# Where the mLSTM's inverse roots are taken, and which rows begin the output projection

## What is computed

```python
ht = mlstm_chunkwise(mq_h, mk_h, mv_h, log_i, log_f)
ht = ht * lax.rsqrt(jnp.mean(ht * ht, axis=-1, keepdims=True) + EPS)
m_out = ht.reshape(B, S, MLSTM_W) * mh_norm_g * jax.nn.sigmoid(mo)
...
a_out = sliding_window_attention(q, k, v, attn_sinks)
y = jnp.concatenate([m_out, a_out], axis=-1)
return y @ w_out
```

## Time and profile before

| | us |
|---|---|
| median of 3 runs | 3037.35 (3036.88 to 3037.41) |
| the profiled execution | 3027.4 |
| its span, first to last instruction | 3025.7 |
| TensorE busy | 2869.6 |
| VectorE busy | 1771.5 |
| ScalarE busy | 1181.9 |
| GpSimd busy | 202.1 |

### The profile page before, as it was taken

How to read it: one execution, slowest core, us unless ns; L and a number is a source line. 1 busy time by engine, 2 the same in 40 slices (tenths; PEclk the granted TensorE clock), 3 DMA queues, 4 the chain that set the end, 5 groups by cost and what they waited for, 6 DMA issues and landing times. The chain is left out here.

```text
span 3025.7 us, 35464 instructions
## 1 busy us (share of the span) xinstructions
PE 2869.6 (95%) x14392; PEld 2397.6 (79%) x14392; DVE 1771.5 (59%) x2588; ACT 1181.9 (39%) x1737; POOL 202.1 (7%) x206
## 2 busy tenths in 40 slices
PE   8979999999988999989969999999999988899999
PEld 6637888878456888879945899999999965688887
DVE  6666766677557767657567565425534127565463
ACT  5254524434444424342245443213323235453342
POOL 1112000020112000000021100000000002100001
PEclk9989999999989999999989999999999999999999
DMA  5302333333112243325630112121121221222322
GB/s 198 104 2 90 111 118 114 95 115 123 49 36 84 94 140 95 118 68 187 234 96 26 66 56 64 53 74 63 61 58 63 63 84 43 94 88 86 110 88 80
DMA packets 84178, 271.47 MB, mean 90 GB/s; under 512 B 9264, under 2 KB 12208, under 8 KB 83632
## 3 DMA queue, kind: packets, MB, share of 16 engines
q1 hardware_dynamic: 84016, 269.21, 27.6%
HBM read 267.08 MB, written 2.10 MB: 89 GB/s over the span
## 5 line engine op out<-in xcount | busy, mean ns | idle before, releaser
L921 PE MATMUL PS<-HH,WH 128*128 128x512 f32 (+1 forms) x3032 | 1004.2, 368 | 56.0 <-DVE HL L566 20.9
L921 PE MATMUL PS<-HL,WH 128*128 128x512 f32 (+1 forms) x3032 | 997.4, 366 | 0.0
L921 PE MATMUL PS<-HH,WL 128*128 128x512 f32 (+1 forms) x3032 | 997.1, 366 | 0.0
L777 DVE TENSOR_TENSOR WL<-STAGE,WH 128x1024 fp32r<-128x1024 f32 (+2 forms) x420 | 482.6, 1150 | 518.5 <-ACT WH L771 518.0
L921 PEld LDWEIGHTS PS<-HH,WH 128*128 128x128 f32 x3032 | 562.5, 189 | 138.8 <-DVE HL L566 28.9
L771 ACT ACTIVATE WH<-STAGE 128x1024 fp32r<-128x1024 f32 (+2 forms) x420 | 407.9, 973 | 658.7 <-DMA STAGE<-in_w_down 275.4
L921 PEld LDWEIGHTS PS<-HH,WL 128*128 128x128 f32 x3032 | 562.8, 189 | 65.7
L921 PEld LDWEIGHTS PS<-HL,WH 128*128 128x128 f32 x3032 | 563.2, 189 | 65.0 <-issue 1.4
L921 PE MATMUL PS<-GH,WH 128*128 128x512 f32 (+1 forms) x880 | 294.7, 367 | 0.0
L921 PE MATMUL PS<-GL,WH 128*128 128x512 f32 (+1 forms) x880 | 294.7, 367 | 0.0
L921 PE MATMUL PS<-GH,WL 128*128 128x512 f32 (+1 forms) x880 | 294.6, 367 | 0.0
(11 more groups left out here) (236 smaller groups left out, 2564.6 us busy)
## 6 DMA issues: line engine op xcount, KB each, us to landing
STAGE<-in_w_up SPq DMA_DIRECT2D x176, 512.0 KB, 3.5
MODBUF<-in_w_mod SPq DMA_DIRECT2D x96, 512.0 KB, 4.2
STAGE<-in_w_in SPq DMA_DIRECT2D x84, 512.0 KB, 3.6
STAGE<-in_w_down SPq DMA_DIRECT2D x64, 384.0 KB, 3.1
STAGE<-in_w_down SPq DMA_DIRECT2D x64, 320.0 KB, 2.9
STAGE<-in_w_out SPq DMA_DIRECT2D x32, 512.0 KB, 4.5
BM<-in_na_bias SPq DMA_DIRECT2D x24, 256.0 KB, 3.1
CR<-in_const_ret SPq DMA_DIRECT2D x2, 1664.0 KB, 8.8
```

Source lines behind the costliest of these rows:

```text
L777: dve.tensor_tensor(WL[unit.slot][:, 0:size], STAGE[unit.slot][:, 0:size], WH[unit.slot][:, 0:size].bitcast(F32), ALU.subtract).then_inc(w ...
L921: ins = pe.matmul(self.acc(tile, col, tn), w[:, c:c + P], r[:, k, t0:t0 + tn], start=(k == 0 and m == 0), stop=(k == seg.kc - 1 and m == 2))
```

## The change

`CopyHead` gives way to `MixHead`. Inside `mix1` the steps that took the roots, spread them, multiplied by gain and gate (DVE) and by the numerator (POOL) are gone, the mixer has 20 steps instead of 22, and ACT's queue ends with a load of the table set of the logarithm. In the output projection's head, ACT takes Ln and Exp once over all 128 partitions; TensorE spreads four rows after chunk 2 of the first three tiles; DVE does the gain and also the product with the numerator, head by head. The eight chunks begin with attention's four rows, of which three are made in the mixer and the fourth in the head; the weight rows are reordered on the host to match. `NUM` moves to the rows of `Z1` that held the queries and keys before their convolution. In step 3 DVE does `weigh` ahead of `normed(0)`.

```diff
@@ -353,7 +353,7 @@
         class Head:
-            begins = False
+            begins = ready = False
             def __init__(self, hi, lo, tokens):
@@ -384,34 +384,74 @@
             def pool(self, pool):
                 pass
-        class CopyHead(Head):
-            def __init__(self, src, chunks, hi, lo, tokens):
-                super().__init__(hi, lo, tokens)
-                self.src, self.chunks = src, chunks
+        class MixHead(Head):
+            begins = ready = True
+            def __init__(self, vec, hi, lo):
+                super().__init__(hi, lo, SEQ)
+                self.vec = vec
             def copied(self, act, c):
-                n = self.tokens
-                act.activation(self.hi[:, c, 0:n], self.src[:, self.chunks[c], 0:n], ACT.Copy).then_inc(h_hi.sem, 1)
+                act.activation(self.hi[:, c, :], Z1[:, ROWS1[c], :], ACT.Copy).then_inc(h_hi.sem, 1)
             def low(self, dve, c):
-                n = self.tokens
                 self.wait_hi(dve, c)
-                dve.tensor_tensor(self.lo[:, c, 0:n], self.src[:, self.chunks[c], 0:n],
-                                  self.hi[:, c, 0:n].bitcast(F32), ALU.subtract).then_inc(h_lo.sem, 1)
+                dve.tensor_tensor(self.lo[:, c, :], Z1[:, ROWS1[c], :], self.hi[:, c, :].bitcast(F32),
+                                  ALU.subtract).then_inc(h_lo.sem, 1)
             def act(self, act):
-                for c in range(4, DC):
-                    self.copied(act, c)
+                act.activation(MEAN2, MEAN2, ACT.Ln, scale=float(D // P)).then_inc(head_ln.sem, 1)
+                self.copied(act, 3)
+                act.wait_ge(head_ln.sem, head_ln.at(1))
+                act.activation(MEAN2, MEAN2, ACT.Exp, scale=-0.5).then_inc(head_rstd.sem, 1)
+                for h in range(4):
+                    act.wait_ge(head_out.sem, head_out.at(h + 1))
+                    self.copied(act, 4 + h)
                 for u in range(3, self.run.ring):
                     self.run.split_high(act, u)
             def dve(self, dve):
-                for c in range(4, DC):
-                    self.low(dve, c)
+                def gain(h):
+                    dve.wait_ge(head_ps.sem, head_ps.at(h + 1))
+                    if later(h - 1):
+                        dve.wait_ge(head_out.sem, head_out.at(h - 1))
+                    dve.scalar_tensor_tensor(out=HG[h % 2], in0=PS[2 + h // 2][:, h % 2 * SEQ:h % 2 * SEQ + SEQ],
+                                             scalar=self.vec[:, V1_MH + h:V1_MH + h + 1], in1=Z1[:, O1 + h, :],
+                                             op0=ALU.mult, op1=ALU.mult).then_inc(hg_done.sem, 1)
+                def out(h):
+                    dve.wait_ge(hg_done.sem, hg_done.at(h + 1))
+                    dve.tensor_tensor(Z1[:, V1 + h, :], NUM[:, h, :], HG[h % 2], ALU.mult).then_inc(head_out.sem, 1)
+                self.low(dve, 3)
+                gain(0)
+                out(0)
+                for h in range(1, 4):
+                    gain(h)
+                    self.low(dve, 3 + h)
+                    out(h)
+                self.low(dve, 7)
                 for u in range(3, self.run.ring):
                     self.run.split_low(dve, u)
+            def begin(self, pe, seg):
+                first = seg.tiles[0:3]
+                for k in range(DC):
+                    if k == 3:
+                        pe.wait_ge(head_rstd.sem, head_rstd.at(1))
+                        for h in range(4):
+                            pe.matmul(PS[2 + h // 2][:, h % 2 * SEQ:h % 2 * SEQ + SEQ],
+                                      CST1[:, C1_SELB + h * P:C1_SELB + h * P + P], MEAN2,
+                                      start=True, stop=True).then_inc(head_ps.sem, 1)
+                    self.wait_lo(pe, k)
+                    for tile in first:
+                        self.run.pe_chunk(pe, tile, k)
         class RetentionHead(Head):
             begins = True
@@ -1039,7 +1079,9 @@
             if any(seg.prep for _, segments in parts for seg in segments):
                 done(qk_own=4, conv_done=12, qk_done=4, gate_ps=2, gate_in=2, abs_done=1, exp1_done=1, ln_done=1, cum_done=2, g_done=1,
                      m_done=1)
-            if parts[0][0].begins:
+            if parts[0][0].ready:
+                done(head_ln=1, head_rstd=1, head_ps=4, hg_done=4, head_out=4)
+            elif parts[0][0].begins:
                 done(mean_ps=3, centred=3, group_sq=3, var_ps=3, group_ln=3, group_rstd=3, group_out=6, gate_done=1)
...
         h1 = region(o_h, 2 * DC * TOK * 4)
         h1("ROWS_LO", [P, 4, SEQ])
         MXB = h1("MXB", [P, 4, SEQ])
-        h1("ROWS_HI", [P, 4, SEQ])
-        NUM = h1("NUM", [P, 4, SEQ])
+        h1("ROWS_HI", [P, 8, SEQ])
+        NUM = Z1[:, Q1:Q1 + 4, :]
         VT = h1("VT", [P, 4, SEQ])
         WT = [h1(f"WT{i}", [P, SEQ]) for i in range(2)]
         PT = [h1(f"PT{i}", [P, SEQ]) for i in range(2)]
...
+        head_ln, head_rstd, head_ps, hg_done, head_out = (
+            S(n) for n in ("head_ln", "head_rstd", "head_ps", "hg_done", "head_out"))
+        ROWS1 = [AQ1, AQ1 + 1, AQ1 + 2, AQ1 + 3, V1, V1 + 1, V1 + 2, V1 + 3]
...
             U = 4 * NB
             LAG = 3
-            steps = range(U + 6)
-            spread = {11: 0, 12: 1, U + 3: 2, U + 4: 3}
+            steps = range(U + LAG + 1)
...
             rotated_at = {-1: (0, 1), 0: (2, 3), 1: (4,)}
-            order = [("scores", 0)]
-            for s in steps:
-                order += [("scores", s + 1)] if s + 1 < U else []
-                order += [("spread", spread[s])] if s in spread else []
-            turn_of = {job: i for i, job in enumerate(order)}
...
-                    def wait_c(job):
-                        if later(turn_of[job] - 1):
-                            kind, x = order[turn_of[job] - 2]
-                            if kind == "scores":
-                                pe.wait_ge(p_done.sem, p_done.at(x + 1))
-                            else:
-                                pe.wait_ge(hg_done.sem, hg_done.at(x + 1))
                     def key_scores(m):
                         h, i = divmod(m, NB)
                         r = half(h % 2)
-                        wait_c(("scores", m))
-                        pe.matmul(c_bank(("scores", m))[:, 0:SEQ - i * P], QK[r, 2 + h // 2, i * P:i * P + P],
+                        if later(m - 1):
+                            pe.wait_ge(p_done.sem, p_done.at(m - 1))
+                        pe.matmul(C_PS[m % 2][:, 0:SEQ - i * P], QK[r, 2 + h // 2, i * P:i * P + P],
                                   QK[r, h // 2, i * P:SEQ], start=True, stop=True).then_inc(c_ps.sem, 1)
...
-                    def spread_rows(h):
-                        pair = half(h // 2)
-                        pe.wait_ge(hrstd.sem, hrstd.at(h // 2 + 1))
-                        wait_c(("spread", h))
-                        pe.matmul(c_bank(("spread", h)), CST1[pair, C1_SELB + h * P:C1_SELB + h * P + P], MEAN2[pair, :],
-                                  start=True, stop=True).then_inc(c_ps.sem, 1)
...
                             mean_square(s // NB - 1)
-                        if s in spread:
-                            spread_rows(spread[s])
...
-                    def rstd(p):
-                        rows = MEAN2[half(p), :]
-                        act.wait_ge(v_done.sem, v_done.at(p + 1))
-                        act.activation(rows, rows, ACT.Ln, scale=float(D // P)).then_inc(hln_done.sem, 1)
-                        act.wait_ge(hln_done.sem, hln_done.at(p + 1))
-                        act.activation(rows, rows, ACT.Exp, scale=-0.5).then_inc(hrstd.sem, 1)
...
                             squares(s // NB - 1)
-                        if s in (10, U + 2):
-                            rstd(s // (U + 2))
                         if U - 4 <= s < U - 4 + READY:
                             ahead.split_high(act, s - U + 4)
-                        if U - 3 <= s <= U:
-                            if s < U - 1:
-                                act.wait_ge(head_out.sem, head_out.at(s - U + 4))
-                            else:
-                                act.wait_ge(o_done.sem, o_done.at(NB * (s - U + 2)))
-                            ahead.first_head.copied(act, s - U + 3)
+                        if U - 3 <= s < U:
+                            c = s - U + 3
+                            act.wait_ge(o_done.sem, o_done.at(NB * (c + 1)))
+                            ahead.first_head.copied(act, c)
+                    act.preload_act_table_set("natural_log")
...
-                    def head(h):
-                        pool.wait_ge(hg_done.sem, hg_done.at(h + 1))
-                        pool.tensor_tensor(Z1[:, V1 + h, :], NUM[:, h, :], HG[h % 2], ALU.mult).then_inc(head_out.sem, 1)
...
                             sinks(a)
-                        if s in (13, 14, U + 4, U + 5):
```

(43 more changed lines are left out.)

## The result

**3005.93 us** median (3004.39 to 3006.99, 4 runs) against 3037.11 for the kernel before (3036.18 to 3037.41, 4 runs) in the same comparison: ratio 0.9896, 95% interval 0.988 to 0.9911. That is 31.2 us less; forecast were 22.8, with 3008 as the low end of the range. The direction held, the size was 8.4 us short.

What follows compares the result with a forecast made beforehand. In the mixer a ring of DVE, ACT and TensorE was taken as the bound, behind the first group TensorE; 6.7 + 6.2 + 4.2 + 5.3 + 0.4 = 22.8 us gave 3004.6 profiled, 3014.5 median, range 3008 to 3024.

Steps and rivals of the forecast that it cites:

- weigh 11 to 15: Mixer steps between those DVE weigh starts: 25.32 us in layer 0 and 24.77 in layer 1 would become 18.6.
- weigh 15 to first copy-out: Mixer's tail plus output projection's first tiles: 4.2 us gained in layer 0, 5.3 in layer 1, to 36.9 us.
- order swap: Mixer step 3, weigh ahead of normed(0): DVE's weigh no longer delays the next mask, 0.2 us a layer.
- The middle: Mid-mixer steps without the root, gain rows and POOL products fall to quiet pace: 6.7 us in layer 0, 6.2 in layer 1.
- Rival (c): Mid-mixer gives back less, step 12 to 13 staying near 7.5 us: 3019, or 3023 with head stalls; chance 0.25.
- The tail: Mixer's end: everything between attention's last store and POOL's last product goes; projection starts 0.75 us after block end, at 217.9.
- drain: Table load at block's end: skill's extra 1.38 us was not charged, only 1.28; with it, 20.0 instead of 22.8 us.
- The spreads' price: Projection's head, before chunk 3: four fp32 spreading matmuls on TensorE cost 3.6 us, not hidden.
- (d): Gain is eaten: mixer's ring takes no room back, head stalls cost 2.5 us a layer: 3033; chance 0.04.
- (e): Slower: head starves TensorE, which stays at 1.2 GHz for the whole group: 3046; chance 0.03.
- The head: Output projection's first three tiles: kept at 17.7 us, first 5.0 at 1.2 GHz, plus 3.6 for spreads.
- Rival (b): TensorE doesn't fall to 1.2 GHz between mixer and projection: 2.4 us more a layer, 3010; chance 0.18.

Runs made afterwards that it cites:

- experiment 5: Changed kernel with ACT's Ln and Exp and their two table loads back in step 10, result unused: 3015.51 us.
- experiment 6: Changed kernel with two useless POOL products a layer back in steps 13 and 14: 3009.24 us.
- experiment 7: Changed kernel with each of the head's four spreading matmuls issued twice: 3015.64 us.
- experiment 8: Changed kernel with the head's four products on POOL instead of VectorE: 3006.84 us.
- experiments 2 and 4: 2: kernel before with six useless fp32 matmuls a layer in the tail, 3029.3 us; 4: changed kernel with two more table loads ending ACT's block, 3014.75 us.
- experiment 9: Changed kernel with useless fp32 matmuls in TensorE's remaining holes in the mixer: 3002.85 us, repeated 3004.61 us.

## Why the prediction was right or wrong

The terms against the two profiles of before and the three of after (first matmul, stores and copies as in the timelines):

| | forecast | measured |
|---|---|---|
| weigh 11 to 15, layer 0 | 6.7 | 6.7, 7.3 (25.32, 25.93 to 18.65) |
| the same, layer 1 | 6.2 | 6.1, 6.7 (24.77, 25.34 to 18.65) |
| weigh 15 to first copy-out, layer 0 | 4.2 | 4.6 (mean of 41.1, 41.3 less mean of 35.3, 37.2, 37.1) |
| first to third copy-out, layer 0 | not priced | 1.1 (9.79, 9.74 to 8.75, 8.69, 8.65) |
| weigh 15 to first copy-out, layer 1 | 5.3 | 8.3 (mean of 42.2, 43.6 less mean of 35.4, 34.2, 34.2) |
| order swap, both layers | 0.4 | 0.5 (weigh 2 to 4: 11.52 and 11.65 to 11.31) |
| sum, of the means | 22.8 | 27.9 |

**The middle: right**, step by step, and its chosen value of 18.6 to 0.05 us. How it is made up is partly different: the clock after the stall and ACT's queue make 3.9 and 5.1 (experiment 5), POOL's products 0.94 (experiment 6), which the prediction had at 0.85 for one step and more inside another; what is left, 1.8 to 2.4 us in layer 0 and 0.1 to 0.7 in layer 1, would be the spreads, the gain rows and what they do together, which no run took alone. Rival (c) is refuted: step 12 to 13 is 5.11 or 5.12 us in all six layers. (Its 4.4 us would be 4.7 by its own 7.5 and 5.11 and the 7.40 of layer 1.)

**The tail: right.** Everything between store and product went. The step from block end to first matmul was 0.51 us and not 0.75. The drain that the Trainium skill, "ScalarE: Activation LUTs", section "What ACT_TABLE_LOAD costs", adds to a load isn't to be seen here either: the load ends at 213.98, ACT's Ln of the next block starts at 214.31 and TensorE at 214.49, and each load in the longer hole adds just 1.29 us (3.33 less 0.75, by two).

**The spreads' price: right.** 3.60 us, wholly exposed (experiment 7), no wait behind them, products hidden on either engine (experiment 8). Rivals (d) and (e) are refuted.

**The head: the step that failed.** "I keep 17.7", with the first 5.0 us at 1.2 GHz. Measured, the first 5.0 us ran at 2.4 GHz in four of six heads. The slow stretch wasn't the head's own: it followed from TensorE's idle time in the tail, which the change takes away (experiments 2 and 4). Rival (b), given 0.18, is what came in layer 1 in all three profiles, 2.4 us by its own sum and some 2.5 measured; in layer 0 it came in one of three, in the others 1.6 us of it stayed. The head grew by 0.9 us in layer 1 and by 3.0 in layer 0 (mean of 17.71, 18.00 to mean of 19.83, 21.39, 21.41) for the 3.6 of the sum, so this step is worth 3.3 of the 5.1 us by which the table's sum was too small. Of the rest 1.1 is VectorE's lateness at layer 0's first copy-out, given back by the third, and 0.5 the middle, priced from a quick execution. The argument against (b), that TensorE fell to 0.52 in the tail though it was busy, was sound for the tail (it still falls there: see the last section) and was wrongly carried over to the head. The Trainium skill, "TensorE: Matmul & The Clock Gate", section "Why this matters for your kernels", whose rule is that longer idle gaps bring the clock down, gave the better answer for this step. The slow stretches that stay it doesn't explain: TensorE idles for 1.09 us before the head's first matmul, and nowhere for more than 1.7 us in the changed kernel's mixer.

**What stays open.** The terms add up to 27.9 us; the medians of the three comparisons give 31.2, 29.3 and 30.0. The rest, 1.4 to 3.3 us, is within the scatter of single executions (3004 to 3011 and 3028 to 3041), and no stretch was found that holds it. The profiled executions can't place it, for they are only 22.7 us apart on the mean (3025.7 and 3034.2 against 3005.3, 3009.1 and 3007.4): the part behind layer 1's third copy-out, the same code in both kernels, took 2120.6 and 2122.6 us in the two of before and 2124.2 to 2126.1 in the three of after, and over all 14 profiles 2120.6 to 2126.9 whatever the edit. That the sum was made on a quick execution (3027.4) and carried to the median by a constant did no harm to the terms of the sum, but the range was too narrow at its low end: its (b) counted 2.4 us a layer for the head's clock and nothing for the slow clock within the tail, while in layer 1 tail and head gave 6.8 to 9.4 us for the 5.3 forecast.

## What to carry to other kernels

Price a stall of TensorE with what runs slowly after it: here each hole of some 9 us cost 2.3 to 2.8 us more behind it, and useless matmuls in it gave back 7.8 us of 3037 with no other change. A short serial chain that all engines wait for belongs beside a stretch of independent matmuls (here 27, 6.2 us) that hides it; what then stays on TensorE, the spreads, is paid in full. When one profiled execution lies apart from the median, take a second one before setting the range.

## What the hardware showed that was not expected

The granted clock falls in the tail of both kernels though TensorE is mostly busy: in the changed kernel's layer 0 it stands at 0.50 from 200.5 to 210.7, with TensorE busy for 8.92 of 10.20 us, behind a stretch at 1.00 that was no busier as a whole (184.04 to 199.03: 12.29 of 14.99 us). Right ahead of the fall it was sparser, 3.72 of 5.20 us, with a wait of 1.48 us. Windows of the changed kernel, and the matmul behind that wait:

```profile
184.04:199.03 14.99, 12.29 (x64) 5.60 (x64) 10.50 (x25) 10.52 (x24) 1.07 (x5) 1.00 0.00 1
...
195.30:200.50 5.20, 3.72 (x32) 2.40 (x32) 3.98 (x10) 2.94 (x7) 0.20 (x2) 1.00 0.00 2
200.50:210.70 10.20, 8.92 (x38) 3.97 (x34) 9.18 (x22) 6.36 (x18) 0.00 (x0) 0.50 0.00 0
```

```profile
199.36 0.49 PE L1347 MATMUL PS<-PT,VT 128*128 128x128 f32 x2 [1.48 <-DVE PT L1526]
```

Weigh 15 to the end of the last store takes 14.2 to 14.7 us in the four layers where 3.4 us of it are at half clock (the filled kernel of experiment 9), and 14.6 to 16.0 in the other 24, where it is 6.8 or 10.2 us. So this low clock costs little, up to 1.8 us, and what beside it makes the difference no run says. And the same program falls to 1.2 GHz in different steps from one execution to the next: layer 0's weigh 3 to 5 took 13.5 us in the second profile of the changed kernel and 11.6 in the first. With the fillers of experiment 9 the tail's slow stretch is 3.4 us instead of 10.2, so what TensorE does in that stretch bears on its length; why it falls there at all, behind a wait of under 2 us, no experiment here says.
